# The outset of a two-layer hybrid encoder: the first two projection units worked side by side over the input tiles

## The chip, the cores and the metric

The kernel runs on one core of a Trainium2 chip. The metric is the device time of one execution in microseconds; three runs of the kernel before gave 1383.38, 1383.63 and 1385.27 us, median 1383.63. The kernel is written in Bass: each engine has its own instruction list, and semaphores order the engines among each other. Engines are called as the profile calls them: PE is TensorE, DVE is VectorE, ACT is ScalarE, POOL is GpSimd, SP is SyncE, which here issues all transfers.

## The reference

Two layers, each of them: RMS norm of the hidden state, one combined input projection to 9216 columns, a group of eight HGRN2 heads and a group of eight differential attention heads on its columns, one output projection, residual add. 16 meta tokens stand before the 512 tokens, so 528 tokens run through. The part that the outset of the kernel computes, cut to what matters:

```python
def rmsnorm(x, g):
    ms = jnp.mean(x * x, axis=-1, keepdims=True)
    return x * lax.rsqrt(ms + NORM_EPS) * g

h = jnp.concatenate([meta, x], axis=1)            # 528 tokens x 1024
for l in range(2):
    u = rmsnorm(h, norm_g[l])
    p = u @ w_in[l]                               # 1024 x 9216
    hq, hf_f, hf_b, hi, hgt, aq, ak, av, agt = jnp.split(p, split_idx, axis=-1)
    o_h = hgrn2_mixer(hq, hf_f, hf_b, hi, hgt, lbs[l], hg_norm_g[l])
    o_a = diff_attention_mixer(aq, ak, av, agt, diff_lambda[l], diff_subln_g[l], l, cos, sin)
    h = h + jnp.concatenate([o_h, o_a], axis=-1) @ w_out[l]
return rmsnorm(h, final_norm_g)[:, N_META:]
```

`lbs` comes from a softmax over the logits `hg_lb_logits`, and a scalar of the attention from exponents of `diff_lambda`.

## The kernel before

The hidden state lies transposed in `h`: eight tiles (`KT` = 8) of 128 channels by 528 tokens. The weights are packed into units. A unit is 128 output columns of a projection, 1024 x 128 values or 0.5 MB: eight blocks of 128 x 128, one for each tile. Layer 0 begins with the units of the first HGRN2 head in the order `zf`, `zb`, `q`, `v`, `g`; they are units 0 to 4 here.

Products are taken in three passes to keep the precision of float32. Both operands are cut into a high part in the format fp32r and a low remainder. ACT writes the high parts: `cut_u_high` for a tile of the input (`u_hi`, with the gain of the norm as scale), `cut_high` for the weights of a unit (`w_hi`). DVE writes the low parts, `cut_u_low` (`u_lo`) and `cut_low` (`w_lo`), and waits for ACT's high part each time. Raw weights have two buffers (`N_RAW` = 2), cut weights three (`N_CUT` = 3). `piece(l, i, k)` on PE multiplies block k of unit i with tile k: three products (`w_hi` with `u_hi`, `w_hi` with `u_lo`, `w_lo` with `u_hi`) on each of two token halves of 264, six matmuls, added up in a bank of PSUM. The result of unit t goes to `proj[t % 2]`, that of unit 2 (`THIRD_UNIT`) to the bank `pair`.

The root of the norm isn't known when the projection begins, since it is a factor for each token and can be multiplied in later. ACT squares the eight tiles (`square_h`, written to `decay`), DVE adds seven of them up in six steps (`add_squares`, in `mixed_t`), PE sums over the channels with a matrix of ones (`sum_squares`, into `far`), ACT takes the root (`root`) and DVE the reciprocal (`invert_roots`, `rms_inv`). Then `evacuate` on DVE multiplies the result of a unit by `rms_inv` on its way out of PSUM. This frees the bank: `evacuated[t % 2]` is what PE waits for before it starts unit t + 2 in the same bank. Unit 3 thus waits for the evacuation of unit 1.

Nothing is scheduled by a planner here: each engine runs the list as it is written. In the kernel before, SP issues the gains, tile 0, the weights of unit 0, tiles 1 to 7, the weights of unit 1, six small parameter transfers (`consts_in`), the weights of unit 2, masks and rotary tables, and then further weights; from unit 2 on, `load(u)` waits until the low cut of unit u - 2 is done. PE warms up with 18 matmuls on ones (36 in the profile, which counts the two passes of a float32 matmul), runs unit 0 and then unit 1 whole, and inserts `sum_squares` behind piece 5 of unit 1. DVE cuts tile 0, unit 0, tiles 1 to 7 and unit 1, adds the squares, prepares exponents (`prepare_exponents`) and cuts unit 2. Behind the reciprocal DVE evacuates unit 0, cuts unit 3, and evacuates unit 1.

Lines of the kernel before that the rows name: L957 high cut of weights, L965 square, L976 high part of a tile, L982 root, L1397 low cut of weights, L1412 addition of squares, L1417 reciprocal, L1424 low part of a tile, L1462 evacuation, L1932 projection matmul, L1962 and L1965 sums of squares, L1975 warm-up, L784 and L842 input tiles, L799 weights, L2149 a product of the HGRN2 heads that needs their states, which DVE writes on L1687.

## Time and profile before

| | |
|---|---|
| Median of three runs | 1383.63 us (1383.38 to 1385.27) |
| Time of the profiled execution | 1386.13 us |
| Its span, first to last instruction | 1384.3 us |
| PE busy | 1369.8 us, 99% |
| DVE busy | 1045.7 us, 76% |
| ACT busy | 837.9 us, 61% |
| Granted PE clock, mean | 0.998 |
| Bytes moved by DMA | 140.41 MB, 101 GB/s |

The profile is one execution, slower than the median of the runs; its spans and starts are counted from its first instruction. PE is busy nearly all the time. Its idle time lies in a few places: ahead of the first matmul of the warm-up (0.98 us), ahead of unit 0 (0.81) and ahead of unit 1 (0.64) at the outset, and before the line L2149 once in each layer (2.31 and 1.95 us). A busy PE counts as busy at the lower clock too, so the granted clock has to be read beside it. Matmuls overlap at their ends, so the distance between starts, and not the duration of one, says how fast the stream runs.

### The profile page before, as it was taken

To read this page: it belongs to the slowest core of one execution; us is meant where nothing else is said; L and a number is where in the kernel's file an instruction comes from. 1 tells how busy PE (TensorE), PEld (TensorE's weight loads), DVE (VectorE), ACT (ScalarE), POOL (GpSimd) and SP (SyncE) were. 2 spreads that over 40 slices of the span, in tenths; PEclk is the share of its full clock that TensorE was granted. 3 is DMA by queue.
4 is the path that set the end of the run, shared out by engine and by line. 5 is a ranking of instruction groups with operands and counts; after the bars stand their busy time and mean duration, and the time that the engine had idled before them with its cause. 6 is when DMAs were issued, how large, how long until landed. Compare 5 with 4: busy or idle time off the path is not lost.

```text
span 1384.3 us, 32303 instructions
## 1 busy us (share of the span) xinstructions
PE 1369.8 (99%) x13108; PEld 1291.5 (93%) x13108; DVE 1045.7 (76%) x1765; ACT 837.9 (61%) x1802; POOL 180.8 (13%) x158
## 2 busy tenths in 40 slices
PE   9999999999999999999999999999999999999998
PEld 9999999999999999999998888888888899999987
DVE  6888778888646777877667878888886478888864
ACT  7666666665434665666555667666664456666654
POOL 1111222220000000000001122222210000000100
PEclk9999999999999999999999999999999999999999
DMA  5333322332324333333233232333333233334332
GB/s 187 115 101 93 108 87 85 108 108 80 98 63 129 99 102 100 100 92 101 69 107 104 89 108 85 108 107 108 108 89 103 88 105 107 108 108 114 113 96 76
DMA packets 76340, 140.41 MB, mean 101 GB/s; under 512 B 9504, under 2 KB 39456, under 8 KB 76192
## 3 DMA queue, kind: packets, MB, share of 16 engines
q1 hardware_dynamic: 76192, 138.35, 33.1%
q8 instruction: 104, 1.70, 0.5%
q14 instruction: 44, 0.36, 0.1%
HBM read 112.36 MB, written 17.30 MB: 94 GB/s over the span
## 4 chain that ended last, share of the span: by engine, by line
PE 90%; DVE 5%; issue 2%; ACT 2%; DMA 1%; SPq 0%; DVEq 0%; ACTq 0%
PE proj L1932 65%; PE far L2196 5%; PE pair L2179 3%; PE pair L2181 3%; PE far L2213 2%; PE pair L2065 1%; PE far L2198 1%; PE far L2149 1%; PE far L2150 1%; PE pair L1932 1%; PE pair L2131 1%; PE far L2153 1%; DVE w_lo L1397 1%; PE pair L2138 1%; PE far L2065 1%
## 5 line engine op out<-in xcount | busy, mean ns | idle before, releaser
L1932 PE MATMUL proj<-u_hi,w_hi 128*128 128x264 f32 (+1 forms) x1960 | 478.6, 312 | 2.6 <-DVE w_lo L1397 1.5
L1932 PE MATMUL proj<-u_hi,w_lo 128*128 128x264 f32 (+1 forms) x1960 | 458.1, 302 | 0.0
L1932 PE MATMUL proj<-u_lo,w_hi 128*128 128x264 f32 (+1 forms) x1960 | 458.0, 302 | 0.0
L1932 PEld LDWEIGHTS proj<-u_hi,w_hi 128*128 128x128 f32 x1960 | 314.7, 189 | 20.1 <-DVE w_lo L1397 1.8
L1932 PEld LDWEIGHTS proj<-u_hi,w_lo 128*128 128x128 f32 x1960 | 313.9, 188 | 13.5
L1932 PEld LDWEIGHTS proj<-u_lo,w_hi 128*128 128x128 f32 x1960 | 314.0, 188 | 10.6
L1397 DVE TENSOR_TENSOR w_lo<-w_raw,w_hi 128x1024 fp32r<-128x1024 f32 x178 | 226.1, 1270 | 34.5 <-ACT w_hi L957 34.4
L1205 ACT ACTIVATE decay<-pair,neg_max 128x528 f32<-128x528 f32 (+1 forms) x144 | 100.5, 698 | 203.3 <-DVE neg_max L1786 203.2
L957 ACT ACTIVATE w_hi<-w_raw 128x1024 fp32r<-128x1024 f32 x178 | 186.8, 1050 | 48.1 <-PE proj L1932 45.0
L1786 DVE TENSOR_REDUCE neg_max<-pair 128x1 f32<-128x528 f32 (+1 forms) x144 | 101.5, 705 | 92.0 <-PE pair L2181 90.8
L897 POOL TENSOR_TENSOR mix_lo<-mixed_t,mix_hi 128x528 fp32r<-128x528 f32 (+1 forms) x32 | 49.9, 1560 | 473.6 <-ACT mix_hi L1252 473.6
L1932 PE MATMUL proj<-mix_hi,w_hi 128*128 128x264 f32 (+1 forms) x364 | 99.5, 329 | 0.0
L1932 PE MATMUL proj<-mix_lo,w_hi 128*128 128x264 f32 (+1 forms) x364 | 96.2, 320 | 0.0
L1932 PE MATMUL proj<-mix_hi,w_lo 128*128 128x264 f32 (+1 forms) x364 | 96.2, 320 | 0.0
L1656 DVE TENSOR_TENSOR ops<-ops,totals 128x528 f32<-128x528 f32 (+1 forms) x96 | 69.5, 724 | 28.1 <-ACT decay L1123 23.0
L913 POOL TENSOR_SCALAR gate_f<-stage 128x528 f32<-128x528 f32 (+1 forms) x32 | 52.2, 1631 | 224.9 <-ACT stage L1055 224.9
L2196 PE MATMUL far<-v_rows,cols 128*128 128x128 f32 x576 | 76.7, 276 | 0.0
L2179 PE MATMUL pair<-k_stack,q_stack 128*128 128x264 f32 x288 | 76.2, 285 | 0.1
L2181 PE MATMUL pair<-k_low,q_stack 128*128 128x264 f32 x288 | 76.2, 285 | 0.0
L2196 PEld LDWEIGHTS far<-v_rows,cols 128*128 128x128 f32 x576 | 71.2, 191 | 1.7
L1665 DVE TENSOR_TENSOR ops<-ops,totals 128x528 f32<-128x528 f32 (+1 forms) x96 | 69.8, 727 | 0.0
L1932 PEld LDWEIGHTS proj<-mix_hi,w_lo 128*128 128x128 f32 x364 | 60.2, 188 | 5.0
(257 smaller groups left out, 2243.8 us busy)
## 6 DMA issues: line engine op xcount, KB each, us to landing
w_raw<-w_units SPq DMA_DIRECT2D x178, 512.0 KB, 3.5
v_scratch<-blocks SPq DMA_DIRECT2D x128, 64.0 KB, 2.0
v_rows<-v_scratch SPq DMA_DIRECT2D x32, 256.0 KB, 2.8
o_scratch<-blocks SPq DMA_DIRECT2D x104, 64.0 KB, 2.6
q_stack<-gate_f SPq DMA_DIRECT2D x32, 132.0 KB, 2.4
k_stack<-k_stack SPq DMA_DIRECT2D x32, 132.0 KB, 2.4
o_rows<-o_scratch SPq DMA_DIRECT2D x14, 256.0 KB, 3.4
ops<-o_scratch SPq DMA_DIRECT2D x12, 256.0 KB, 2.7
```

Of the source, the lines that this page charges most:

```text
L897: pool.tensor_tensor(mix_lo[:, n % 8, ts], mixed_t[:, ts], mix_hi[:, n % 8, ts].bitcast(f32), ALU.subtract)\
L913: pool.tensor_scalar(gate_f[:, d, ts], stage[:, use % 2, 0, ts], F_FLOOR, None, ALU.max)\
L957: act.activation(w_hi[:, u % N_CUT, :, :], w_raw[:, u % N_RAW, :, :], ACT.Copy)\
L1205: act.activation(two(decay[0:rows, 2 * (i % 2) + comp, :]), pair[0:rows, :, both], ACT.Exp, bias=neg_max[0:rows, i % 2, comp:comp + 1], ac ...
L1397: dve.tensor_tensor(w_lo[:, u % N_CUT, :, :], w_raw[:, u % N_RAW, :, :], w_hi[:, u % N_CUT, :, :].bitcast(f32), ALU.subtract).then_inc(lo_ ...
L1656: dve.tensor_tensor(keys, keys, facing_totals(m, KF), ALU.mult).then_inc(k_widened, 1)
L1665: dve.tensor_tensor(queries, queries, facing_totals(m, QB), ALU.mult).then_inc(qk_ready, 1)
L1786: dve.tensor_reduce(neg_max[0:rows, i % 2, comp:comp + 1], pair[0:rows, :, both], axis=mybir.AxisListType.XY, op=ALU.max, negate=True)\
L1932: ins = pe.matmul(out, w, x[:, tile, cols_n], start=(k == 0 and p == 0), stop=(k == last_k and p == 2))
L2179: pe.matmul(pair[0:rows, b, both], q_stack[:, comp, cs], k_stack[:, comp, keys], start=True, stop=False)
L2181: ins = pe.matmul(pair[0:rows, b, both], q_stack[:, comp, cs], k_low[:, comp, keys], start=False, stop=True)
L2196: pe.matmul(meta[:, 0:P], cols[:, kk, :], v_main(kk), start=(kk == 0), stop=False)
```

## The change

The change touches the outset of layer 0 alone.

- The weights of units 0 and 1 are loaded in two halves each, blocks 0 to 3 and blocks 4 to 7 (`FIRST_K` = 4), and cut in halves (`cut_first_high`, `cut_first_low`). SP's order is: gains, tile 0, first halves of units 0 and 1, tiles 1 to 3, second halves of units 0 and 1, tiles 4 to 7, weights of unit 2, parameters, masks and tables, further weights.
- PE runs units 0 and 1 side by side: for each tile k, piece k of unit 0 and piece k of unit 1. `sum_squares` stands behind piece 1 of unit 2.
- ACT squares tiles 0 to 3 between the high parts of tiles 4 to 7, then cuts unit 2 high, then squares tiles 4 to 7. DVE puts three of the additions between the low parts of tiles 5 to 7, cuts unit 2 low, and then adds the rest.
- The parameters wait, behind the weights of unit 2, for the low cut of unit 0.

```diff
--- before.py
+++ after.py
@@ -72,6 +72,7 @@
 
 EARLY_TILES = 4
 EARLY_K = KT - 1
+FIRST_K = KT // 2
 
 
 def layer_units():
@@ -488,6 +489,9 @@
         x_in = [sem(f"x_in{k}") for k in range(KT)]
         gain_in = sem("gain_in")
         raw_in = [sem(f"raw_in{i}") for i in range(N_RAW)]
+        first_half_in = [sem(f"first_half_in{i}") for i in range(N_RAW)]
+        first_hi_cut = sem("first_hi_cut")
+        first_lo_cut = sem("first_lo_cut")
         out_stored = sem("out_stored")
         ones_set = sem("ones_set")
         pads_set = sem("pads_set")
@@ -779,10 +783,7 @@
 
             def load(u):
 
-                if u == 1:
-                    for k in range(1, KT):
-                        sp.dma_start(h[:, k, :], x_t[:, k, :]).then_inc(x_in[k], 16)
-                if u == N_RAW:
+                if u == N_RAW + 1:
                     for dst, src in ((ident[:, :], identity), (lb[:, :, :], lb_logits), (g_hg[:, :], hg_gain),
                                      (g_at[:, :], at_gain), (g_final[:, :], final_g),
                                      (lam_in[:, :, :, :], lambdas)):
@@ -840,7 +841,12 @@
 
             sp.dma_start(g_in[:, :, :], norm_g).then_inc(gain_in, 16)
             sp.dma_start(h[:, 0, :], x_t[:, 0, :]).then_inc(x_in[0], 16)
-            u = 0
+            for part, arrived in ((slice(0, FIRST_K), first_half_in), (slice(FIRST_K, KT), raw_in)):
+                for u in range(N_RAW):
+                    sp.dma_start(w_raw[:, u, part, :], w_units[u][:, part, :]).then_inc(arrived[u], 16)
+                for k in range(max(part.start, 1), part.stop):
+                    sp.dma_start(h[:, k, :], x_t[:, k, :]).then_inc(x_in[k], 16)
+            u = N_RAW
             for l in range(DEPTH):
                 u = loads_until(u, l * LAYER_STEPS - 1)
                 write_values(l * HEADS)
@@ -956,6 +962,13 @@
                     act.wait_ge(unit_done, u - N_CUT + 1)
                 act.activation(w_hi[:, u % N_CUT, :, :], w_raw[:, u % N_RAW, :, :], ACT.Copy)\
                     .then_inc(hi_cut, 1)
+
+            def cut_first_high(u, part):
+
+                act.wait_ge((raw_in if part else first_half_in)[u], 16)
+                ks = slice(part * FIRST_K, (part + 1) * FIRST_K)
+                act.activation(w_hi[:, u, ks, :], w_raw[:, u, ks, :], ACT.Copy)\
+                    .then_inc(hi_cut if part else first_hi_cut, 1)
 
             def square_h(n, k):
 
@@ -1256,13 +1269,15 @@
             load_root_table()
             for k in range(KT):
                 cut_u_high(0, k)
-                if k == 0:
-                    cut_high(0)
-            cut_high(1)
-            for k in range(KT):
+                if k in (0, FIRST_K - 1):
+                    for u in range(N_RAW):
+                        cut_first_high(u, int(k > 0))
+                if k >= FIRST_K:
+                    square_h(0, k - FIRST_K)
+            for u in range(N_RAW, N_CUT):
+                cut_high(u)
+            for k in range(KT - FIRST_K, KT):
                 square_h(0, k)
-            for u in range(2, N_CUT):
-                cut_high(u)
             root(0)
             for l in range(DEPTH):
                 if l == 0:
@@ -1396,6 +1411,16 @@
                 dve.wait_ge(hi_cut, u + 1)
                 dve.tensor_tensor(w_lo[:, u % N_CUT, :, :], w_raw[:, u % N_RAW, :, :],
                                   w_hi[:, u % N_CUT, :, :].bitcast(f32), ALU.subtract).then_inc(lo_cut, 1)
+
+            def cut_first_low(u, part):
+
+                if part:
+                    dve.wait_ge(hi_cut, u + 1)
+                else:
+                    dve.wait_ge(first_hi_cut, u + 1)
+                ks = slice(part * FIRST_K, (part + 1) * FIRST_K)
+                dve.tensor_tensor(w_lo[:, u, ks, :], w_raw[:, u, ks, :], w_hi[:, u, ks, :].bitcast(f32),
+                                  ALU.subtract).then_inc(lo_cut if part else first_lo_cut, 1)
 
             def cut_after(l, units):
 
@@ -1822,14 +1847,16 @@
             after(step(dve.tensor_scalar(g_in[:, :, :], g_in[:, :, :], math.sqrt(D_MODEL), None, ALU.mult)))
             for k in range(KT):
                 cut_u_low(0, k)
-                if k == 0:
-                    cut_low(0)
-            cut_low(1)
-            for k in range(1, KT - 1):
+                if k in (0, FIRST_K - 1):
+                    for u in range(N_RAW):
+                        cut_first_low(u, int(k > 0))
+                if k > FIRST_K:
+                    add_squares(0, k - FIRST_K)
+            for u in range(N_RAW, N_CUT):
+                cut_low(u)
+            for k in range(KT - FIRST_K, KT - 1):
                 add_squares(0, k)
             prepare_exponents()
-            for u in range(2, N_CUT):
-                cut_low(u)
             for l in range(DEPTH):
                 invert_roots(l)
                 for i in range(len(HG_TILES)):
@@ -1907,8 +1934,11 @@
 
                 what, c, j, _ = UNITS[i]
                 t = l * LAYER_UNITS + i
+                if t < N_RAW and k < FIRST_K:
+                    pe.wait_ge(first_lo_cut, t + 1)
+                elif k == (FIRST_K if t < N_RAW else 0):
+                    pe.wait_ge(lo_cut, t + 1)
                 if k == 0:
-                    pe.wait_ge(lo_cut, t + 1)
                     if i == THIRD_UNIT:
                         if l > 0:
                             before_it = (l - 1) * LAYER_UNITS + OUT_C
@@ -2218,10 +2248,14 @@
 
                 if l == 0:
                     warm_up()
-                for i in range(len(HG_TILES)):
+                if l == 0:
+                    for k in range(KT):
+                        for i in range(N_RAW):
+                            piece(l, i, k)
+                for i in range(N_RAW if l == 0 else 0, len(HG_TILES)):
                     for k in range(KT):
                         piece(l, i, k)
-                        if i == 1 and k == (KT - 3 if l == 0 else 1):
+                        if (i, k) == ((N_RAW, 1) if l == 0 else (1, 1)):
                             sum_squares(l)
                 for c in range(HEADS):
                     for s in range(steps_of(c)):
```

Numbers behind a name in the next rows tell buffers apart. On PE, from the first projection matmul on, before (`proj0` is the bank of unit 0; every further piece of unit 0 follows, and unit 1 comes after all eight):

```order
L1932 MATMUL proj0<-u_hi,w_hi 128x264 [waits u_lo_ready,lo_cut]
L1932 MATMUL proj0<-u_hi,w_hi 128x264
L1932 MATMUL proj0<-u_lo,w_hi 128x264 x2
L1932 MATMUL proj0<-u_hi,w_lo 128x264 x2
L1932 MATMUL proj0<-u_hi,w_hi 128x264 [waits u_lo_ready]
```

and of the changed kernel (`proj1` is the bank of unit 1):

```order
L1962 MATMUL proj0<-u_hi,w_hi 128x264 [waits u_lo_ready,first_lo_cut]
L1962 MATMUL proj0<-u_hi,w_hi 128x264
L1962 MATMUL proj0<-u_lo,w_hi 128x264 x2
L1962 MATMUL proj0<-u_hi,w_lo 128x264 x2
L1962 MATMUL proj1<-u_hi,w_hi 128x264 [waits first_lo_cut]
L1962 MATMUL proj1<-u_hi,w_hi 128x264
L1962 MATMUL proj1<-u_lo,w_hi 128x264 x2
L1962 MATMUL proj1<-u_hi,w_lo 128x264 x2
L1962 MATMUL proj0<-u_hi,w_hi 128x264 [waits u_lo_ready,first_lo_cut]
```

Each tile is now followed by a piece of either unit, and the first pieces wait for a half of the cut weights.

On PE, the place of the sums of squares before, between pieces 5 and 6 of unit 1:

```order
L1932 MATMUL proj1<-u_hi,w_lo 128x264 x2
L1962 MATMUL far<-mixed_t,ones 128x264 [waits h_sq_added]
L1962 MATMUL far<-mixed_t,ones 128x264
L1965 MATMUL far<-decay,ones 128x264 [waits h_sq]
L1965 MATMUL far<-decay,ones 128x264
L1932 MATMUL proj1<-u_hi,w_hi 128x264 x2
```

and of the changed kernel, where `pair` is the bank of unit 2:

```order
L1962 MATMUL pair<-u_hi,w_hi 128x264 x2
L1962 MATMUL pair<-u_lo,w_hi 128x264 x2
L1962 MATMUL pair<-u_hi,w_lo 128x264 x2
L1992 MATMUL far<-mixed_t,ones 128x264 [waits h_sq_added]
L1992 MATMUL far<-mixed_t,ones 128x264
L1995 MATMUL far<-decay,ones 128x264 [waits h_sq]
L1995 MATMUL far<-decay,ones 128x264
L1962 MATMUL pair<-u_hi,w_hi 128x264 x2
```

Fourteen pieces stood ahead of the sums before, eighteen stand there now.

On DVE, from the low part of tile 5 to the reciprocal, in the changed kernel (before, all low parts of tiles stood together, then unit 1's cut, all six additions, the exponents and unit 2's cut):

```order
L1449 SCALAR_TENSOR_TENSOR u_lo<-h,g_in,u_hi 128x528 [waits u_hi_ready,x_in5]
L1437 TENSOR_TENSOR mixed_t<-decay 128x528 [waits h_sq]
L1449 SCALAR_TENSOR_TENSOR u_lo<-h,g_in,u_hi 128x528 [waits u_hi_ready,x_in6]
L1437 TENSOR_TENSOR mixed_t<-mixed_t,decay 128x528 [waits h_sq_added,h_sq]
L1449 SCALAR_TENSOR_TENSOR u_lo<-h,g_in,u_hi 128x528 [waits u_hi_ready,x_in7]
L1437 TENSOR_TENSOR mixed_t<-mixed_t,decay 128x528 [waits h_sq_added,h_sq]
L1412 TENSOR_TENSOR w_lo<-w_raw,w_hi 128x1024 [waits hi_cut]
L1437 TENSOR_TENSOR mixed_t<-mixed_t,decay 128x528 [waits h_sq_added,h_sq] x3
```

Three additions moved ahead of the low cut of unit 2 (L1412 in the changed kernel). Behind the reciprocal nothing moved: evacuation of unit 0, low cut of unit 3, evacuation of unit 1.

## Rows read from the trace of the kernel before

**Rows 1.** The page's part 4: shares of the chain by engine, over the whole span.

```profile
PE 90%; DVE 5%; issue 2%; ACT 2%; DMA 1%; SPq 0%; DVEq 0%; ACTq 0%
```

**Rows 2.** Chain of waits, first 90 us: start us, us, what.

```profile
5.51 7.12 DMA w_raw<-w_units
```

**Rows 3.** Timeline of PE at the outset: start us, us, instructions, idle before and releaser.

```profile
6.84 0.61 PE L1975 MATMUL far<-ones 128*128 128x128 f32 x4
8.26 0.51 PE L1932 MATMUL proj<-u_hi,w_hi 128*128 128x264 f32 x2 [0.81 <-DVE w_lo L1397]
9.10 0.41 PE L1932 MATMUL proj<-u_hi,w_hi 128*128 128x264 f32 x2
13.49 0.41 PE L1932 MATMUL proj<-u_hi,w_hi 128*128 128x264 f32 x2
15.02 0.51 PE L1932 MATMUL proj<-u_hi,w_hi 128*128 128x264 f32 x2 [0.64 <-DVE w_lo L1397]
19.70 1.16 PE L1962 MATMUL far<-mixed_t,ones 128*128 128x264 f32 x4
21.39 0.60 PE L1932 MATMUL proj<-u_hi,w_hi 128*128 128x264 f32 x2
28.90 0.41 PE L1932 MATMUL proj<-u_hi,w_hi 128*128 128x264 f32 x2
```

**Rows 4.** Timeline of DVE at the outset.

```profile
5.51 0.77 DVE L1424 SCALAR_TENSOR_TENSOR u_lo<-h,g_in,u_hi 128x528 fp32r<-128x528 f32 x1 [2.97 <-ACT u_hi L976]
8.12 4.84 DVE L1424 SCALAR_TENSOR_TENSOR u_lo<-h,g_in,u_hi 128x528 fp32r<-128x528 f32 x7
15.69 3.96 DVE L1412 TENSOR_TENSOR mixed_t<-mixed_t,decay 128x528 f32<-128x528 f32 x5
22.53 3.45 DVE L1417 RECIPROCAL rms_inv<-rms_inv 128x528 f32<-128x528 f32 x1 [0.57 <-ACT rms_inv L982]
27.77 0.70 DVE L1462 TENSOR_TENSOR stage<-proj,rms_inv 128x528 f32<-128x528 f32 x1
```

**Rows 5.** Timeline of ACT at the outset.

```profile
4.63 0.73 ACT L976 ACTIVATE u_hi<-h,g_in 128x528 fp32r<-128x528 f32 x1 [0.42 <-DMA h<-x_t]
12.65 1.06 ACT L957 ACTIVATE w_hi<-w_raw 128x1024 fp32r<-128x1024 f32 x1 [0.64 <-DMA w_raw<-w_units]
13.61 4.37 ACT L965 ACTIVATE decay<-h 128x528 f32<-128x528 f32 x8
21.79 0.71 ACT L982 ACTIVATE rms_inv<-far,eps_count 128x528 f32<-128x528 f32 x1 [2.85 <-PE far L1965]
24.04 1.05 ACT L957 ACTIVATE w_hi<-w_raw 128x1024 fp32r<-128x1024 f32 x1
```

**Rows 6.** DMA: unit 0's issue and landing; a stretch's busy times; SP's later issues.

```profile
w_raw<-w_units SPq DMA_DIRECT2D x1, 512.0 KB, 4.2
...
8.26:14.40 6.14, 6.12 (x48) 5.91 (x48) 5.36 (x8) 5.21 (x8) 0.00 (x0) 1.00 1.05 380
...
14.99 28.59 SPq L799 DMA_DIRECT2D w_raw<-w_units  x7
```

**Rows 7.** Timeline of PE around its two longest waits.

```profile
337.73 0.40 PE L1932 MATMUL proj<-u_hi,w_lo 128*128 128x264 f32 x2
340.44 0.80 PE L2149 MATMUL far<-v_rows,score 128*128 128x128 f32 x2 [2.31 <-DVE state_f L1687]
343.78 0.39 PE L2153 MATMUL far<-state_b,ops 128*128 128x128 f32 x2
344.01 0.39 PE L2149 MATMUL far<-v_rows,score 128*128 128x128 f32 x2
1031.37 0.49 PE L2149 MATMUL far<-v_rows,score 128*128 128x128 f32 x2 [1.95 <-DVE state_f L1687]
```

**Rows 8.** Windows of 1 us behind those waits: busy times, PEclk, DMA share, GB/s.

```profile
342.00:343.00 1.00, 1.00 (x7) 1.00 (x7) 0.96 (x2) 0.00 (x0) 0.00 (x0) 0.50 0.62 146
1031.00:1032.00 1.00, 0.63 (x5) 0.63 (x6) 1.00 (x2) 0.00 (x0) 0.82 (x1) 1.00 0.93 213
```

## The prediction

> **What bounds the kernel now.** I read the shares of the chain first. TensorE holds 90% of it [rows 1], so the change can only pay where TensorE waits, or where something else ends last. Next comes the chain over the first 90 us. Ahead of the first projection matmuls it runs over the issue of nine transfers, then over the last of them, unit 1's weights: 7.12 us to landing [rows 2], then the high cut on ACT (12.65 [rows 5]), the low cut on DVE, and from 15.02 TensorE alone [rows 3]. Third, TensorE's own timeline shows what that is worth. Its warm-up ends at 7.45 (6.84 + 0.61), and the first piece starts at 8.26 after 0.81 idle. Unit 0 has eight pieces: the second starts at 9.10 and the eighth at 13.49, so a piece takes 0.732, and a ninth could have started at 14.22. It started at 15.02: 0.80 lost. After six pieces of unit 1 come the sums of squares (19.70), 1.69 us until projection goes on (21.39), and unit 3 starts at 28.90 [rows 3]. So all that the outset can give back is 0.8 + 0.8 us and a few tenths.
>
> The fourth view, DVE's timeline, has the second line of work, the one that the change must not lengthen. The sums release the root on ACT at 21.79 [rows 5]; the reciprocal runs 22.53 to 25.98, then the scaling of unit 0, the low cut of unit 3, and the scaling of unit 1 from 27.77 to 28.47 [rows 4]. That last one empties `proj[1]`, and unit 3 on TensorE (start 28.90) may not write this bank before. It is 28.47 - 19.70 = 8.77 us from the start of the sums, and only 0.43 before it is needed. I take this as what decides.
>
> **The change, part by part.**
> *Starting with half of the weights.* The first piece needs tile 0's low cut and one half of unit 0's low cut. Tile 0 is in at 4.63, where ACT starts on it [rows 5]. Its low part runs 5.51 to 6.28 [rows 4]. A whole unit's weights landed 4.2 us after their issue, at 5.8 [rows 6]; a half lands between tile 0 and that. A half's high cut is estimated at 0.72 (0.73 for 528 columns, 1.06 for 1024 [rows 5]) and its low cut at 0.68 (0.70 for 528 columns [rows 4]). With the half in at 5.3 the low cut is done at 6.9, with it in at 5.8 at 7.3; both are before the warm-up's 7.45. The warm-up is not changed, so the first piece starts at 7.3 to 7.45 in place of 8.26: 0.8 to 0.95 earlier, and no more however early the half lands.
>
> *Two units side by side.* Each tile now feeds two pieces, 1.46 us. The tiles land at about 377 GB/s, since the queue moved 380 GB/s from 8.26 to 14.40 [rows 6]: 0.27 MB in 0.72 us. Weights and tiles hold 3.2 MB in either order, so the last arrives at about 12.6 as before, but now it is tile 7. I laid the new order out with the pitches of the rows: 0.68 for a tile's low part (7 in 4.84), 0.62 to 0.68 for its high part, 0.53 for a square (8 in 4.37), 0.6 for half a cut. The low parts of tiles 1, 5 and 7 are ready at 8.2, 13.2 and 15.8; TensorE comes for them at 8.8, 14.6 and 17.6. The second halves of the cuts are ready at 11.3, wanted at 13.2. No wait is left in the sixteen pieces, the 0.80 us is gone. Tile 1 has least cover, 0.6 us; without it the loss is what it comes late.
>
> *Weights of unit 2.* They wait for the second half of unit 0's low cut (10.7), land at about 14.2, are cut high after the fourth square (16.2) and low by 17.6. Unit 2 begins at 19.0. Hidden, with 1.4 us to spare.
>
> *Squares between the tiles, sums later on TensorE.* The additions need the tiles' order on DVE: three of the six stand among the low parts, the other three end at about 19.8, with 0.8 between them (5 in 3.96 [rows 4]). Before they ended at 19.65. The sums now stand behind 18 pieces and not 14. They start at 7.35 + 18 x 0.732 = 20.5 (20.6 if the first piece is again 0.1 longer), so the additions do not hold them up; 0.7 us is their cover. This is 0.8 to 0.9 later than 19.70.
>
> *The parameters later.* Six small transfers with the issue now behind unit 2's: about 11.1 to 14.3. They are wanted at 19.8 for the exponents, five small instructions on DVE, which is then idle until the reciprocal (23.3), so they may take 3.5 us. Masks and tables follow; unit 3's weights leave at about 15.1, as before (14.99 [rows 6]), while ACT cut them high only at 24.04 [rows 5] and now will at about 24.8. I cost it at nothing. If the parameters landed after 22, each us more would be a us of the end.
>
> *The sum.* Unit 3 can start, by the weights and TensorE's own work, at 20.5 + 1.69 + 6 x 0.732 = 26.6: 2.3 us earlier than 28.90. But the bank is free only at 20.5 + 8.77 = 29.3 (29.2 to 29.45). So TensorE will stand idle from about 26.8 to 29.3, some 2.5 us, and unit 3 starts 0.3 to 0.55 later than now. The 1.6 us gained at the front and the 0.3 before the sums come back as this one wait, because moving the sums four pieces back (2.9 us) is more than all that the front gives. DVE and ACT are 0.8 late and TensorE 0.4, so behind this DVE lags 0.4 more; TensorE does not wait for it again in the first 50 us, so I take nothing for it, with 0.4 as the upper bound. Sum: +0.4 us.
>
> **From the span to the time.** The profiled execution took 1386.13 us, 1.83 outside its span, and is 2.50 above the median of 1383.63. Part of that is one event. At 337.73 + 0.40 TensorE ran dry; after 2.31 us it went on at 340.44, and the next eight pairs of matmuls took until 343.78, 0.42 each; the pair after that took 0.23 (to 344.01) [rows 7]. The granted clock reads 0.50 in between, 1.2 GHz [rows 8]. 3.34 us instead of 8 x 0.23: 1.5 us lost. The stall at 1031.37, 1.95 us, kept its clock of 1.00 [rows 7, 8]. One of the three timed runs is 1.64 above the other's median, about as much. I add +0.4 to the median: 1384.0 (to the profiled execution: 1386.5).
>
> **The rule that speaks against.** The new wait of 2.5 us is longer than the one that was followed by the low clock. So the same may happen at 29.3. The Trainium skill, "TensorE: Matmul & The Clock Gate", section "HAM oscillation — how this bites in real kernels", says that a TensorE left idle long enough between bursts is put back to half rate and starts the next burst cold; by it the change costs a second such episode. The trace agrees at 340.44 and not at 1031.37.
>
> The other rule would speak against the halves. "DMA: Bandwidth & Descriptors" of the Trainium skill, section "Anatomy of one DMA — SWDGE (gpsimd) path", puts a fixed 2.0 us on each DMA; an estimate by it, if the two extra transfers paid that one behind the other, is a last tile 4 us later and a time near 1387. In this trace seven tiles are issued one behind the other and the queue still moves 380 GB/s [rows 6], so fixed parts lie beside each other.
>
> **Rivals.**
> A, slower: the new stall brings the clock down. Price 1.5 us [rows 7] on top of 0.4: 1385.5. It decides if the stall is as the one at 338.1 and not as the one at 1029.4; being longer than both speaks for it, that a stall nearly as long passed without speaks against. 0.33.
> B, faster: unit 3 does not wait for the bank, because I misread the second line (a root or reciprocal that starts earlier). Then -2.3: 1381.3. Only the 8.77 us of rows 3 to 5 would have to be wrong; 0.03.
> C, slower: the sums slip because halves or tiles land late or the additions come after 20.5. Each us beyond the cover of 0.7 is a us of the end. With DVE full from 13.7 to 20.5 a delay of 1 to 2 us at the tiles gives +0.7 to +1.7, 1384.7 to 1385.7, and together with A up to 1387. 0.08.
> D, the change doesn't do what it says: the front isn't earlier, since the half of unit 0 lands as late as the whole or behind it. Then the sums start at 21.4, and unit 3 at 30.2: +1.3, 1384.9. 0.03.
> Forecast as summed, 0 to +0.8: 0.53.
>
> **The numbers.** Forecast 1384.0, its own range 1383.4 to 1384.5. The range has to take in A with DVE's 0.4 (1385.9) and the least of C (0.5 more), and on the other side the forecast's 0 with the scatter of the runs (0.25 down), and a third of the way to B: 1382.9 to 1386.4. A change of 0.2%, 2.8 us, is the least that a measurement of this kernel tells from none. No case but a mixture of A and C reaches it, and B lies just within; faster 0.03, same 0.91, slower 0.06.
>
> **What would show it.** In the changed profile: the first projection matmul at 7.3 to 7.5 with no wait ahead, no gap between 7.4 and 20.5; the sums at 20.4 to 20.7; the reciprocal at 23.3; scaling of unit 1 ending at 29.2 to 29.5; TensorE waiting 2.3 to 2.8 us ahead of unit 3, released by DVE's scaling; and a granted clock right behind it of 1.00 (forecast) or near 0.5 for some 3 us (A). It would be wrong if unit 3 started before 28.9, if the sums waited for an addition, or if a wait stood among the first sixteen pieces.

## The result, and the profile of the changed kernel

The changed kernel is slower, by 0.2%: 1388.94 us, the median of 10 runs (1387.73 to 1389.84), beside 1385.65 for the kernel before, 10 runs (1383.38 to 1386.63). The ratio is 1.0026, 95% interval [1.0017, 1.0034]. The forecast of 1384.0 and its range up to 1386.4 were missed. Part of that is the base: 1383.63 was the median of three runs, and over ten runs the kernel before takes 2.0 us more. The change itself costs 3.3 us where 0.4 was forecast.

The profiled execution took 1388.14 us over a span of 1386.4, 2.1 us more than before. The page's part 4, shares of the chain by engine, against [rows 1]:

```profile
PE 90%; DVE 5%; issue 2%; ACT 2%; DMA 0%; SPq 0%; DVEq 0%; ACTq 0%
```

The DMA share has gone from 1% to 0%, but whole per cents say nothing of a change of this size (a profile of the old order below, with a filled wait, shows 0% too). The chain of waits over the first 60 us tells more (start us, us, what):

```profile
2.59 5.84 DMA h<-x_t
...
8.45 0.75 ACT u_hi L989
```

Where the chain ran over 7.12 us of unit 1's weights [rows 2], it now runs over 5.84 us of tile 1. The transfer still decides; it is another one. TensorE's timeline, the places that answer to [rows 3] and the first of [rows 7] (start us, us, instructions, idle before and releaser):

```profile
7.21 0.49 PE L1962 MATMUL proj<-u_hi,w_hi 128*128 128x264 f32 x2
...
8.31 0.51 PE L1962 MATMUL proj<-u_hi,w_hi 128*128 128x264 f32 x2
...
10.21 0.48 PE L1962 MATMUL proj<-u_hi,w_hi 128*128 128x264 f32 x2 [0.90 <-DVE u_lo L1449]
...
20.50 0.41 PE L1962 MATMUL pair<-u_hi,w_hi 128*128 128x264 f32 x2
...
21.96 1.06 PE L1992 MATMUL far<-mixed_t,ones 128*128 128x264 f32 x4
...
30.77 0.48 PE L1962 MATMUL proj<-u_hi,w_hi 128*128 128x264 f32 x2 [2.48 <-DVE stage L1487]
...
342.64 0.49 PE L2179 MATMUL far<-v_rows,score 128*128 128x128 f32 x2 [2.63 <-DVE state_f L1712]
```

The first piece starts at 7.21 without a wait, 1.05 us before the old 8.26. The second comes 0.37 late (8.31; 7.21 + 0.732 is 7.94), the third at 10.21 instead of 9.04. From there fourteen pieces take 10.29 us, 0.735 each, with nothing between them. So the sums start at 21.96, unit 3 at 30.77 behind a wait of 2.48, 1.87 us later than before. From unit 3 to the end of the wait near 340 us it is 311.87 us (342.64 - 30.77), and was 311.54: 0.3 more. 1.87 + 0.33 is 2.2, about the 2.1 of the spans.

Where the 0.3 arise can be read from DVE, whose work ends that wait. First the kernel before, then the changed one: the start of DVE's last stretch ahead of it, and the second shuffle of `stage` in it.

```profile
321.31 0.69 DVE L1656 TENSOR_TENSOR ops<-ops,totals 128x512 f32<-128x512 f32 x1 [1.74 <-ACT decay L1123]
...
331.53 0.76 DVE L1552 STREAM_SHUFFLE stage<-stage 128x528 f32<-128x528 f32 x1
```

```profile
323.19 0.69 DVE L1681 TENSOR_TENSOR ops<-ops,totals 128x512 f32<-128x512 f32 x1 [1.73 <-ACT decay L1136]
...
333.74 0.75 DVE L1577 STREAM_SHUFFLE stage<-stage 128x528 f32<-128x528 f32 x1 [0.36 <-issue]
```

From unit 3 to the start of this stretch it is 292.41 us before (321.31 - 28.90) and 292.42 now (323.19 - 30.77): no lag of DVE is left by then. From there to the end of TensorE's wait it is 19.13 and 19.45. The difference is one gap of 0.36 us, in which DVE waited for nothing that the profile shows ("issue"). It stands at this shuffle in all nine profiles of the changed order and in none of the five of the old one; the stretch takes 19.44 to 19.48 us in the nine and 19.10 to 19.13 in the five.

DVE, for [rows 4]:

```profile
7.57 0.69 DVE L1422 TENSOR_TENSOR w_lo<-w_raw,w_hi 128x512 fp32r<-128x512 f32 x1 [1.15 <-ACT w_hi L970]
...
18.87 2.33 DVE L1437 TENSOR_TENSOR mixed_t<-mixed_t,decay 128x528 f32<-128x528 f32 x3
21.12 0.17 DVE L1361 TENSOR_TENSOR lb_work<-lb 128x16 f32<-128x16 f32 x1
...
24.68 3.45 DVE L1442 RECIPROCAL rms_inv<-rms_inv 128x528 f32<-128x528 f32 x1 [2.30 <-ACT rms_inv L995]
```

The additions end at 21.20 (18.87 + 2.33), 0.76 before the sums: they held up nothing. The exponents start at 21.12 without a wait, so the parameters, issued later, were there. The reciprocal takes 3.45 us as before. ACT, for [rows 5]:

```profile
4.81 0.62 ACT L970 ACTIVATE w_hi<-w_raw 128x512 fp32r<-128x512 f32 x1
6.90 0.63 ACT L970 ACTIVATE w_hi<-w_raw 128x512 fp32r<-128x512 f32 x1 [1.47 <-DMA w_raw<-w_units]
8.45 2.11 ACT L989 ACTIVATE u_hi<-h,g_in 128x528 fp32r<-128x528 f32 x3 [0.92 <-DMA h<-x_t]
```

Unit 0's half is in by 4.8. Unit 1's half comes at 6.9 and tile 1 at 8.4, and ACT waits for both. That is where the start goes. The windows show a part of why; first the kernel before, then the changed one (us, busy times of PE, PEld, DVE, ACT, POOL, granted clock, DMA share, GB/s):

```profile
4.50:5.00 0.50, 0.50 (x5) 0.50 (x4) 0.00 (x0) 0.37 (x1) 0.00 (x0) 1.00 0.99 392
5.00:5.50 0.50, 0.50 (x4) 0.50 (x4) 0.00 (x0) 0.37 (x1) 0.00 (x0) 1.00 1.01 373
5.50:6.00 0.50, 0.50 (x6) 0.50 (x6) 0.49 (x1) 0.11 (x1) 0.00 (x0) 1.00 1.04 355
```

```profile
4.50:5.00 0.50, 0.50 (x5) 0.50 (x4) 0.00 (x0) 0.50 (x2) 0.00 (x0) 1.00 1.19 198
5.00:5.50 0.50, 0.50 (x4) 0.50 (x4) 0.46 (x1) 0.43 (x1) 0.00 (x0) 1.00 0.70 159
5.50:6.00 0.50, 0.50 (x6) 0.50 (x6) 0.50 (x2) 0.00 (x0) 0.00 (x0) 1.00 0.70 215
```

In these 1.5 us 0.56 MB moved before and 0.29 MB now. Missing are 0.27 MB, one tile, or 0.7 us at 377 GB/s. But tile 1 came 1.9 us later than before, at 8.4 and not at 6.5. The other 1.2 us lie in what moved ahead of its last bytes. Up to and with tile 1, SP issues 1.07 MB in either order; when tile 1 landed, the queue had moved 1.35 MB before (207 GB/s over 6.5 us) and 1.79 MB now (212 GB/s over 8.43 us). So transfers issued behind tile 1 went along with it, and in the changed order more of them did. Why they did is not shown.

What the profile of one execution does not show is the spread. The mean granted clock of each run sorts the runs into groups that lie 1.5 to 1.8 us apart, about the price of one stretch at 1.2 GHz (1.5 us in [rows 7]). Over the 18 timed runs of the changed kernel (10 here, 8 below) none had 0.999, 6 had 0.998 (1387.6 to 1388.1) and 12 had 0.997 (1388.7 to 1389.8). The kernel before, in the 74 runs beside the experiments, had 0.999 in 30 (near 1384.1) and 0.998 in 44 (near 1385.9). I read this as one such stretch or none before, and one or two now. It is a reading of the mean clock, and not a count. In the profiles, this one and those below, it fits (none at 0.999 or more, one at 0.998, two at 0.997), but for one that has 0.997 from a single stretch of double length. The profile above is also the slowest of the six runs of its group, and the profile of the first experiment the second slowest of its twelve, so the starts of 21.96 and 22.00 for the sums are late ones. In the three other profiles with the same outset and the same place of the sums they are at 21.03, 21.31 and 21.66.

### The profile page after: what moved, and what is told of

Its sections match the earlier page's. It is cut to its first block, busy times and chain, and to the rows that moved or that the text cites. A ratio compares the mean times of both kernels' runs of the same rounds, so it can differ in the third digit from the quotient of the medians.

```text
span 1386.4 us, 32313 instructions
## 1 busy us (share of the span) xinstructions
PE 1369.5 (99%) x13108; PEld 1291.8 (93%) x13108; DVE 1045.6 (75%) x1767; ACT 837.5 (60%) x1804; POOL 180.8 (13%) x158
## 4 chain that ended last, share of the span: by engine, by line
PE 90%; DVE 5%; issue 2%; ACT 2%; DMA 0%; SPq 0%; DVEq 0%; ACTq 0%
PE proj L1962 65%; PE far L2226 5%; PE pair L2211 3%; PE pair L2209 3%; PE far L2243 2%; PE pair L2095 1%; PE far L2228 1%; PE far L2179 1%; PE far L2180 1%; DVE w_lo L1412 1%; PE pair L2161 1%; PE far L2183 1%; DVE ops L1690 1%; PE pair L2168 1%; PE far L2095 1%
## 5 line engine op out<-in xcount | busy, mean ns | idle before, releaser
L1412 DVE TENSOR_TENSOR w_lo<-w_raw,w_hi 128x1024 fp32r<-128x1024 f32 x176 | 223.6, 1271 | 32.7 <-ACT w_hi L963 32.6
```

What stands on the lines that cost most here:

```text
L1412: dve.tensor_tensor(w_lo[:, u % N_CUT, :, :], w_raw[:, u % N_RAW, :, :], w_hi[:, u % N_CUT, :, :].bitcast(f32), ALU.subtract).then_inc(lo_ ...
```

## The experiments

The first four were run on one chip, the next four on another, the last four on a third. Each ratio is to the kernel before on the same chip, whose medians were 1384.74 (18 runs), 1385.61 (23) and 1385.46 (33); it lies a little off the quotient of the medians. A profile is always one execution.

**The changed kernel again** (no edit), for a profile with two low stretches.

> The changed kernel as it is, a second profile and more timed runs. Theory (the transfers of the outset land late each time): tile 1 lands at 8.2 to 8.6 again, TensorE waits 0.7 to 1.1 us ahead of the second tile's pieces, the sums start at 21.7 to 22.2 and unit 3 at 30.5 to 31.0; time 2.5 to 4 us above the kernel before. Rival (that trace was one bad draw of the transfers): tile 1 lands at 6.5 to 7.2, the sums start at 20.4 to 20.8, unit 3 at 29.2 to 29.5, time 0.4 to 2 us above the kernel before. The clock theory expects, besides, that most timed runs have a mean granted clock 0.001 below that of the kernel before.

Measured: 1389.11 (8 runs), ratio 1.0025 [1.0014, 1.0035]; this execution 1389.80, span 1388.0. Unit 3 on TensorE, then the windows behind it:

```profile
30.81 0.78 PE L1962 MATMUL proj<-u_hi,w_hi 128*128 128x264 f32 x2 [2.49 <-DVE stage L1487]
```

```profile
31.00:32.00 1.00, 1.00 (x5) 1.00 (x6) 0.86 (x8) 0.00 (x0) 0.00 (x0) 0.50 0.80 197
...
34.00:35.00 1.00, 1.00 (x10) 1.00 (x9) 0.41 (x1) 1.00 (x3) 0.54 (x1) 0.97 0.00 0
```

Same wait as in the first profile (2.49 and 2.48), same front, but here the clock is at 0.50 behind it and the span is 1.6 us longer. This is rival A, seen directly: behind the same wait the clock falls in some executions and not in others. The sums started at 22.00 again, so the late transfers were no single draw.

**The old order, unit 0's weights in two halves.**

```diff
+ if u == 0:
+     for part in (slice(0, KT // 2), slice(KT // 2, KT)):
+         sp.dma_start(w_raw[:, u, part, :], w_units[u][:, part, :]).then_inc(raw_in[u], 16)
+     return
```

> The kernel before, with the weights of unit 0 loaded in two transfers of 256 KB, one right behind the other, and cut when both are in. If halves with their rows of 2 KB are slow in themselves, tile 1 lands at 7.5 to 8.5 instead of 6.5 and the rate of the queue falls below 250 GB/s somewhere between 4.5 and 6 us. If what is slow is the order (two units' halves ahead of tile 1, fewer bytes under way), the rate stays above 330 GB/s from 4 us on and tile 1 lands at 6.5 to 7.1. Either way the first projection matmul starts at 8.2 to 8.8 and the time is that of the kernel before within 1 us.

One run: 1386.71, span 1384.9. TensorE's first piece and the sums, then the windows:

```profile
8.65 0.52 PE L1936 MATMUL proj<-u_hi,w_hi 128*128 128x264 f32 x2 [0.49 <-DVE w_lo L1401]
...
19.98 1.16 PE L1966 MATMUL far<-mixed_t,ones 128*128 128x264 f32 x4
```

```profile
4.50:5.00 0.50, 0.50 (x5) 0.50 (x4) 0.06 (x1) 0.30 (x1) 0.00 (x0) 1.00 1.10 277
5.00:5.50 0.50, 0.50 (x4) 0.50 (x4) 0.50 (x1) 0.00 (x0) 0.00 (x0) 1.00 0.73 265
```

Against the profile of the kernel before (392 and 373 GB/s, first piece at 8.26) this looks like a dip of half the depth. But the old order with nothing altered at its outset comes out the same in another execution, that of the run with the wait near 340 us filled, further below:

```profile
8.62 0.51 PE L1932 MATMUL proj<-u_hi,w_hi 128*128 128x264 f32 x2 [1.84 <-DVE w_lo L1397]
```

```profile
5.00:5.50 0.50, 0.50 (x6) 0.50 (x6) 0.50 (x1) 0.00 (x0) 0.00 (x0) 1.00 0.85 327
```

From 4.5 to 6 us 0.43 MB moved here, and 0.46, 0.51 and 0.56 MB in the three profiles with the unaltered old outset. So this run doesn't show that halving unit 0's weights slows the queue, and neither of the two outcomes that were expected came as described (lowest rate 265 GB/s, tile 1 at 7.1).

**Tile 1 between the first halves.**

```diff
+ if u == part.start == 0:
+     sp.dma_start(h[:, 1, :], x_t[:, 1, :]).then_inc(x_in[1], 16)
```

> The changed kernel with tile 1 issued between the first halves of unit 0 and unit 1, nothing else. If late tile 1 is what holds TensorE, and it was late by its place in the queue, it lands at 6.5 to 7.2, and the first half of unit 1 at 7.2 to 8.4, each half a piece's worth nearer to its use: TensorE loses at most 0.6 us in the first four pieces (1.2 to 1.4 in the changed kernel), the sums start at 21.0 to 21.5 and unit 3 at 29.8 to 30.3, time 0.5 to 1 us below the changed kernel. If the queue as a whole has a hole between 4.5 and 6 us, the order inside it does not matter: the last of the first four pieces ends as late, the sums start at 21.7 to 22.2, time the same within 0.4.

Measured: 1389.42 (5 runs), 1.0032 [1.0019, 1.0044]. ACT and TensorE:

```profile
8.02 0.63 ACT L972 ACTIVATE w_hi<-w_raw 128x512 fp32r<-128x512 f32 x1 [2.71 <-DMA w_raw<-w_units]
```

```profile
9.43 0.51 PE L1964 MATMUL proj<-u_hi,w_hi 128*128 128x264 f32 x2 [1.43 <-DVE w_lo L1424]
...
22.05 1.06 PE L1994 MATMUL far<-mixed_t,ones 128*128 128x264 f32 x4
```

Tile 1 came in time, unit 1's half came at 8.0 instead of 6.9, and the sums started at 22.05, as before the edit. Whichever of the two is issued last comes at 8.0 to 8.4, so their order gives nothing, as the second expectation had it.

**The sums behind sixteen pieces, not eighteen.**

```diff
+ if l == 0 and i == N_RAW:
+     sum_squares(l)
```

> The changed kernel with the sums of squares directly behind the sixteen pieces of units 0 and 1, two pieces sooner. Theory (unit 3 starts 8.7 us behind the start of the sums, whatever TensorE does): the sums wait for the last addition and start at 21.2 to 21.3, 0.7 sooner than in the changed kernel, unit 3 starts at 29.9 to 30.1 and TensorE's wait ahead of it stays 2.4 to 2.6 us less what the sums themselves waited (1.6 to 1.9); time 0.7 us less than the changed kernel. Rival (TensorE's own work decides and the wait ahead of unit 3 is something else, the low cut of unit 3 say, that does not hang on the sums): unit 3 starts at 30.6 to 30.9 as before and the time is the same within 0.3.

Measured: 1387.03 (11 runs), 1.0015 [1.0006, 1.0024]. TensorE:

```profile
20.36 1.16 PE L1992 MATMUL far<-mixed_t,ones 128*128 128x264 f32 x4 [0.62 <-DVE mixed_t L1437]
...
29.27 0.49 PE L1962 MATMUL proj<-u_hi,w_hi 128*128 128x264 f32 x2 [0.97 <-DVE stage L1487]
```

Unit 3 follows the sums by 8.91 us, and the wait ahead of it is now 0.97. The median is 2.1 us below that of the changed kernel on the same chip, where 0.7 was expected. Four of the eleven runs had a mean clock of 0.999 and only two 0.997: with the wait short, the second low stretch is gone from most runs, and the expectation had left the clock out. In this execution the transfers also came about 1.1 us sooner than in the first profile (ACT cut unit 1's half at 5.79), so not all of the 1.50 us at unit 3 is the edit's.

**The old order, tiles 1 and 2 ahead of unit 0's weights.**

```diff
+ if u == 0:
+     for k in (1, 2):
+         sp.dma_start(h[:, k, :], x_t[:, k, :]).then_inc(x_in[k], 16)
```

> The kernel before with tiles 1 and 2 issued ahead of unit 0's weights, whole as they were: the first four transfers are 264, 264, 264 and 512 KB, no halves. Theory (the queue's hole near 5 us comes from small transfers at the start, whatever they carry): the rate falls below 300 GB/s somewhere from 4 to 6 us, and unit 0's weights land 0.4 us or more behind the 7.4 that 1.3 MB take at the rate of the kernel before. Rival (it comes from halves with rows of 2 KB): the rate stays above 330 GB/s from 4 us on and the weights land at 7.2 to 7.6. Either way the first projection matmul is 1.5 to 2.5 us later than in the kernel before.

One run: 1389.08. TensorE, then windows at the start and behind the wait:

```profile
10.97 0.51 PE L1935 MATMUL proj<-u_hi,w_hi 128*128 128x264 f32 x2 [3.54 <-DVE w_lo L1400]
```

```profile
4.50:5.00 0.50, 0.50 (x5) 0.50 (x4) 0.00 (x0) 0.50 (x1) 0.00 (x0) 1.00 0.99 337
5.00:5.50 0.50, 0.50 (x4) 0.50 (x4) 0.24 (x1) 0.12 (x1) 0.00 (x0) 1.00 0.80 298
...
13.00:14.00 1.00, 1.00 (x7) 1.00 (x6) 1.00 (x2) 1.00 (x3) 0.00 (x0) 0.50 1.01 384
```

The figures are those that the theory named: 298 GB/s at the lowest, and unit 0's weights 6.0 us after their issue, at 8.6, where 7.4 was worked out from the rate. But from 4.5 to 6 us 0.47 MB moved, which is within what the unaltered old outset moved (0.46 to 0.56), so this run doesn't show that small transfers at the front slow the queue. What stays is that a transfer landed later than its place in the queue and the rate say. The new wait of 3.54 at the first piece brought the low clock as well.

**Both first halves in one transfer of 512 KB.**

```diff
+ sp.dma_start(w_raw[:, 0:N_RAW, part, :],
+              w_units[0:N_RAW, :, part, :].rearrange("u p k m -> p u k m")).then_inc(arrived[0], 16)
```

> The changed kernel with the first halves of units 0 and 1 in one transfer of 512 KB (still rows of 2 KB). If the hole comes from small transfers, it closes: more than 300 GB/s from 4.5 to 6 us, both halves land at 5.7 to 6.2, tile 1 at 6.5 to 7.2, the sums start at 20.5 to 21.0, unit 3 at 29.2 to 29.7, and the time is 1.0 to 1.6 us below the changed kernel. If it comes from rows of 2 KB, the rate falls below 250 GB/s again, tile 1 lands at 8 or later and the time stays within 0.5 us of the changed kernel.

Measured: 1388.74 (11 runs), 1.0025 [1.0016, 1.0034]. Windows and TensorE:

```profile
4.50:5.00 0.50, 0.50 (x7) 0.50 (x7) 0.03 (x1) 0.33 (x1) 0.00 (x0) 1.00 1.10 330
5.00:5.50 0.50, 0.50 (x7) 0.50 (x6) 0.50 (x1) 0.00 (x0) 0.00 (x0) 1.00 0.86 285
```

```profile
7.54 0.51 PE L1965 MATMUL proj<-u_hi,w_hi 128*128 128x264 f32 x2 [0.83 <-DVE w_lo L1425]
...
20.78 1.06 PE L1995 MATMUL far<-mixed_t,ones 128*128 128x264 f32 x4
...
29.60 0.48 PE L1965 MATMUL proj<-u_hi,w_hi 128*128 128x264 f32 x2 [2.49 <-DVE stage L1490]
```

With one larger transfer the rate is 330 and 285, tile 1 landed at 7.0, no wait stands among the tiles' pieces, and sums (20.78) and unit 3 (29.60) come 0.3 behind where the prediction had put them (20.5 and 29.3). So what held the sums back in the first profile was the late landing. In time it is worth much less than the 1.0 to 1.6 us expected: the ratio is that of the changed kernel, the two clock groups lie 0.2 to 0.3 lower by their means, and five of eleven runs are in the lower one. This fits the first two profiles being late ones.

**The wait ahead of unit 3 filled** with matmuls whose result nobody reads.

```diff
+ if l == 0 and i == THIRD_UNIT + 1:
+     pe.wait_ge(root_ready, 1)
+     for j in range(8):
+         pe.matmul(main[:, j % 4 * P:(j % 4 + 1) * P], ones[:, :], ones[:, :], start=True, stop=True)
```

> The changed kernel with eight matmuls on ones, some 2.1 us, that TensorE runs in its wait ahead of unit 3; their result is never read. Theory (the wait lets the clock fall in most executions): unit 3 starts where it started, 30.6 to 31.0, the granted clock behind it is always 1.00, and the median of the timed runs is 0.8 to 1.6 us below that of the changed kernel, with the upper of its two groups of times gone. Rival (the clock there has no part in the time): the median stays within 0.3 us.

Measured: 1388.38 (9 runs), 1.0023 [1.0013, 1.0032].

```profile
27.48 1.95 PE L2259 MATMUL far<-ones 128*128 128x128 f32 x16
...
30.12 0.48 PE L1962 MATMUL proj<-u_hi,w_hi 128*128 128x264 f32 x2 [0.70 <-DVE stage L1487]
```

Idle time ahead of unit 3 is 0.70, and only 2 of 9 runs still have a clock of 0.997, after 12 of 18. Few as these runs are, over the three edits that shorten this wait (sums sooner, this one, cut sooner) it is 8 of 29. So TensorE's idle time here was the cause of the second stretch in most runs. The median falls by 0.6 to 0.7 only, since the runs with one stretch lie 0.5 to 0.6 higher than those of the changed kernel; I can't say why.

**Unit 3's weights cut before the reciprocal.**

```diff
+ cut_high(N_CUT)
  root(0)
  ...
  prepare_exponents()
+ cut_low(N_CUT)
```

> The changed kernel with both cuts of unit 3 ahead of the root and the reciprocal, in time in which ACT and DVE only wait for the sums; the evacuations of units 0 and 1 follow each other. Theory (unit 3 waits for the evacuation of unit 1, at the end of a chain from the sums): the chain from the start of the sums to unit 3 is 7.6 to 7.8 us in place of 8.8, TensorE waits 1.2 to 1.5 us in place of 2.5, and the time falls by 1.1, and by up to 1 more where the shorter wait no longer costs clock. Rival (the low cut of unit 3 itself, or something else than the evacuation, decides): unit 3 starts at 30.5 to 31.0 again and the time is the same within 0.4.

Measured: 1387.88 (9 runs), 1.0019 [1.0009, 1.0029]. DVE, then TensorE:

```profile
27.24 1.32 DVE L1489 TENSOR_TENSOR stage<-proj,rms_inv 128x528 f32<-128x528 f32 x2
```

```profile
28.71 0.48 PE L1966 MATMUL proj<-u_hi,w_hi 128*128 128x264 f32 x2 [1.35 <-DVE stage L1489]
```

The chain from the sums (21.03) to unit 3 is 7.68 us, 1.1 shorter, as expected for a low cut taken out of it. The median is 1.1 to 1.2 us below the two of the changed kernel, the least that was expected (1.1, and up to 1 more from the clock). The clock gave little here: in this profile the low clock near 340 us lasted about twice as long as elsewhere (0.52 at 340:341, still 0.57 at 346:347), and two runs took over 1390.

The last four ask what is left when the clock is taken out.

**The old order with the wait near 340 us filled**, and the same wait in layer 2.

```diff
+ if c == HG_HEADS - 1:
+     for j in range(7):
+         pe.matmul(main[:, j % 4 * P:(j % 4 + 1) * P], ones[:, :], ones[:, :], start=True, stop=True)
+ pe.wait_ge(states_ready, g + 1)
```

> The kernel before with seven matmuls on ones (some 1.8 us, result never read) in TensorE's wait for the states of head 7, once in each layer; nothing else. Clock theory: the kernel before falls into two groups, near 1384.1 at a mean clock of 0.999 and near 1385.9 at 0.998, by whether the wait near 340 us is followed by the low clock; filled, only the lower group is left: median 1383.8 to 1384.4, all runs at 0.999. Rival (the groups come from something else): both groups stay, median 1385 to 1386.

Measured: 1384.67 (11 runs, 1383.97 to 1385.02), 0.9996 [0.9988, 1.0005].

```profile
337.59 1.72 PE L2148 MATMUL far<-ones 128*128 128x128 f32 x14
...
340.04 0.49 PE L2152 MATMUL far<-v_rows,score 128*128 128x128 f32 x2 [0.73 <-DVE state_f L1687]
```

All eleven runs have a mean clock of 0.999 or more, and their spread is 1.05 us where the kernel before has 3 (33 runs). So the low stretch hung on TensorE standing idle in this wait. The gain is 0.8 us against the median, within what the interval allows for none. The runs lie some 0.5 above the undisturbed ones of the kernel before, and 0.3 above the range expected; why is open.

**The changed kernel with both waits filled** (the edit of the run with the wait ahead of unit 3 filled, and this one).

> The changed kernel with matmuls on ones both in its wait ahead of unit 3 (eight) and in the waits for the states of head 7 (seven). No wait of TensorE over 1 us is left behind the warm-up, so by the clock theory nearly all runs are at 0.999. The time left over g3_before_filled is then the part of the change that is not clock: by the traces 1.9 to 2.3 us (late transfers, sums four pieces later). Median 1385.7 to 1386.6. Rival (the clock has no part, all of the 3.3 to 4.4 us are geometry): median 1387.3 or more with g3 at 1384.

Measured: 1386.21 (11 runs), 1.0009 [1.0000, 1.0018]; all with a clock of 0.999 or more.

```profile
30.48 0.48 PE L1962 MATMUL proj<-u_hi,w_hi 128*128 128x264 f32 x2 [0.70 <-DVE stage L1487]
...
342.63 0.49 PE L2182 MATMUL far<-v_rows,score 128*128 128x128 f32 x2 [1.07 <-DVE state_f L1712]
```

Against the old order with the same fill this is 1.54 us (1386.21 - 1384.67), the part of the change that is not the clock, and less than the 1.9 to 2.3 that the profiles had led me to expect. For the rest this is an estimate, with the mean clock read as above: 44 low stretches in 74 runs are 0.59 a run, one and 12/18 are 1.67 a run; 1.07 more of them at 1.6 us are 1.7 us. 1.5 + 1.7 is 3.2, for a measured 3.3.

**The old order, filled, with unit 3's weights cut sooner** (the edit of the cut above), to see whether the evacuation of units 0 and 1 sets the wait near 340 us.

> The kernel before with two edits: seven matmuls on ones (some 1.8 us, result never read) in TensorE's wait for the states of head 7 in each layer, and unit 3's two cuts ahead of root and reciprocal. Compare with g3_before_filled, which has the first edit alone. DVE evacuates unit 1 some 0.5 us sooner (27.9), TensorE starts unit 3 at 28.9 as before. Theory (the line that ends at the evacuation of unit 1 also sets the wait near 340 us): that wait ends 0.3 to 0.5 us sooner and the time is 0.3 to 0.5 below g3. Rival (behind unit 3 TensorE's own pace sets it): the wait near 340 ends at the same distance from the start of unit 3 (311.5), time the same within 0.2.

Measured: 1384.71 (11 runs), 0.9997 [0.9988, 1.0005]: the same as without the edit. DVE emptied both banks by 27.95, 0.3 sooner than in the kernel with the fill alone (28.25) although the sums began 0.4 later; unit 3 started at 29.05, and the wait near 340 ended 311.45 us behind it, against 311.36 with the fill alone. Evacuating sooner doesn't shorten it. In the changed order the same edit left it at 2.62 us, with the gap of 0.36 us in DVE. So the evacuation is not the reason for the longer wait.

**All the mends together on the changed kernel**: both first halves in one transfer, sums behind sixteen pieces, unit 3 cut sooner, wait near 340 filled.

> The changed kernel with what the earlier runs point to: first halves in one transfer, sums directly behind the sixteen pieces, unit 3's cuts ahead of the root, and the matmuls on ones at head 7. Theory (chain from the last addition over the sums to the evacuation of unit 1 decides, the rest is clock): sums start at 20.2 to 21.0 with a wait for the last addition, unit 3 7.7 us later at 27.9 to 28.7, a wait ahead of it below 0.5, clock 1.00 throughout; time 1383.2 to 1384.2, at or just below the kernel before with the same filling (g3). Rival (side by side order costs something that these edits do not touch): time above g3 by 1 us or more.

Measured: 1385.44 (11 runs), 1.0005 [0.9996, 1.0014].

```profile
21.82 1.06 ACT L966 ACTIVATE w_hi<-w_raw 128x1024 fp32r<-128x1024 f32 x1 [3.42 <-DMA w_raw<-w_units]
```

ACT stood 3.42 us for unit 3's weights and only then took the root that it stands ahead of, so unit 3 started 9.04 us behind the sums (19.97 and 29.01), not 7.7. It ends 0.8 above the old order with the fill alone: the expected 1383.2 to 1384.2 was missed, and the rival's 1 us was not quite reached. No form of the new order beat the old one, and the old one filled is not shown to beat the kernel before.

## Why the prediction was wrong

**Right.** The front (in the first profile): the first piece at 7.21, without a wait (7.3 to 7.45 forecast). The 0.80 us that unit 1's weights cost is gone. The chain from the sums to unit 3 is 8.81 us (8.77). A wait of 2.48 stands ahead of unit 3, released by DVE's scaling (2.5). Parameters, unit 2's weights and the order of the additions cost nothing, and neither does the lag of DVE behind unit 3: it takes up work from ACT near 321 us, 292.4 us behind unit 3 in both kernels. A low stretch costs 1.6 (1.5). In all nine profiles of the changed order it is DVE's scaling that unit 3 waits for, so the second line of work decides, and the gain at the front comes back as one wait. The last tile landed at about 13.8 (issued at 7.2, 6.6 us under way), 1.2 later than forecast and not the 4 us of the estimate by the Trainium skill, "DMA: Bandwidth & Descriptors", section "Anatomy of one DMA — SWDGE (gpsimd) path"; that section is about transfers that GpSimd issues, and here SP issues them.

**Wrong, step by step.**
1. "The tiles land at about 377 GB/s". That rate was read from 8.26 to 14.40 [rows 6], when a deep queue of transfers was under way, and used for 4.5 to 6 us. There it was 159 to 215, which makes tile 1 0.7 us late. It also took for granted that the bytes land in the order of issue, and transfers issued behind tile 1 moved ahead of its end, which is the other 1.2 us. Unit 1's half came at 6.9 and cost 0.37, tile 1 at 8.4 instead of 6.5 and cost 1.17, and "No wait is left in the sixteen pieces" fell with it. The sums began at 21.96: 2.26 later than before instead of 0.8 to 0.9, and unit 3 1.87 later instead of 0.3 to 0.55. The runs as a whole lose less than this profile (1.5 us without the clock). This is rival C, which was given 0.08 and was priced rightly (+0.7 to +1.7); the 0.6 us of cover for tile 1 should have been held against a landing time that the trace had never shown for such a transfer. Both first halves in one transfer put the sums at 20.78, so the rest of the sum up to unit 3 holds.
2. Rival A, the clock, was given 0.33. Two low stretches came in 12 of 18 runs, and in 2 of 9 once this wait was filled. The profile before had one wait of 2.31 followed by a fall and one of 1.95 that was not, and 2.5 is beyond the first; that evidence was worth more than one in three.
3. A term that was missing. The wait near 340 us grew: it is 2.27 to 2.31 in the three profiles of the old order without a fill there and 2.62 to 2.65 in all seven of the changed order, and unit 3 to its end took 0.3 more. "I take nothing" for DVE's lag was right, as said; what was paid is the gap of 0.36 us in DVE's own list, for which the sum had no term. No term had the clock behind that wait either: with the wait ahead of unit 3 at 1.35 or less (sums sooner, that wait filled, cut sooner), 22 of 29 runs still had a low stretch, against 44 of 74 before. These shares are too near each other to be called different; if they are, it is 0.16 x 1.6 = 0.3 us of the 1.7.
4. The base. By their times, the three runs happened to hold two without a low stretch; the forecast said that one of them was 1.64 above, "about as much", but built on the median all the same.

With the measured terms the sum is 1.5 us for a later unit 3 and the gap in DVE (by the two filled kernels), 1.7 for the clock, on 1385.65: 1388.9. In one reading the prediction slipped without harm: ahead of unit 1's weights the chain runs over ten issues, not nine.

**Open.** What makes DVE's gap of 0.36 us. The changed order has two more instructions on DVE (1767 against 1765 on the page), and the gap stands at the same place whatever the timing; whether the one brings the other was not tried. And why the early transfers land late: from 4.5 to 6 us 0.29 to 0.42 MB moved in the seven profiles with two separate first halves of units 0 and 1, and 0.43 to 0.56 in the seven others. Size, order and the bytes under way changed together, and no run parts them. From one execution to the next the same outset moved a lot: in the six profiles with that of the changed kernel unit 1's half landed between 5.8 and 7.4 and tile 1 between 7.3 and 8.5.

## What to carry to other kernels

Don't take a queue's rate from its full stretch for its first two microseconds: when an early start hangs on small transfers, bound their landing by the nearest first transfers in the trace, don't count on the bytes landing in the order of issue, and see how much cover is left. When work is moved so that one engine's gain is returned at a single wait, price that wait twice, by its length and by the TensorE clock behind it, and compare it with the waits after which the clock did and did not fall. When a wait far from the change grows, follow the engine that ends it instruction by instruction: here the cause stood in one line of DVE's timeline. And take the base from the groups that the runs fall into, not from the median of three.

## What the runs showed of the hardware

TensorE's clock was at 0.50 behind waits of 2.27 to 2.65 us near 340 us in every profile where that wait was not filled, in none where fourteen short matmuls cut it to 0.7 or 1.1, and never behind the second layer's wait of 1.95 to 2.05. Behind the wait of 2.48 to 2.49 ahead of unit 3 it fell in one of the two profiles of the changed kernel, and in neither of the two others with that wait (tile 1 sooner, first halves in one). The same wait thus had either outcome. By the mean clock this holds for the wait near 340 us too: 30 of the 74 runs of the kernel before have 0.999. The Trainium skill, "TensorE: Matmul & The Clock Gate", section "HAM oscillation — how this bites in real kernels", tells of bursts that start cold behind idle stretches; these runs agree in that each fall to 0.50 named above stood behind idle time of TensorE, and add that filling such a wait with idle matmuls made the time steadier (a spread of 1.05 us instead of 3) rather than clearly shorter.

From 4.5 to 6 us the queue's lowest rate in half a microsecond was 159 and 177 GB/s in the two profiles of the changed kernel, against 355, 275 and 274 in the three with the unaltered old outset. A transfer did not land when the bytes up to its own had moved: for tile 1 these were 1.07 MB, and it landed at 1.35 MB in the kernel before and at 1.79 MB in the changed one.

DVE stood for 0.36 us between two instructions of its own list with no wait that the profile shows, at one place, in all nine profiles of the changed order and in none of the old one.
